# Norm and rotation of queries and keys made within the compression of cached keys, gates at the projection's head, shorter rings

## The reference

```python
def layer_forward(x, p_l, pos, z_prev0, wkv0, attend, lp):
    h = rmsnorm(x, lp['attn_norm'])
    z = h @ lp['w_in']
    o_r, wkv, shift = rwkv_mix(z[..., :RWKV_COLS], z_prev0, wkv0, lp)
    qn, qr, kvc, kvs, kvw, gates = nsa_project(z[..., RWKV_COLS:RWKV_COLS + NSA_COLS], pos, lp)
    o_n = attend(qn, qr, kvc, kvs, kvw, gates)
    ...
    x = x + peer_ffn(rmsnorm(x, lp['ffn_norm']), lp)

def nsa_project(zn, pos, lp):
    ...
    gates = jax.nn.sigmoid(zn[..., NSA_WIDTH + 6 * KV_WIDTH:].reshape(B, T, NSA_HEADS, N_NSA_BRANCH))
    qn = rmsnorm(q, lp['q_norm'])
    qr = rope(qn, pos)
    def prep(kvb, gk):
        return jnp.stack([rope(rmsnorm(kvb[:, :, 0], gk), pos), kvb[:, :, 1]], axis=2)
    return qn, qr, kv[:, :, 0], prep(kv[:, :, 1], lp['k_norm'][1]), prep(kv[:, :, 2], lp['k_norm'][2]), gates

def compress(kv_raw, lp):      # for the prompt's raw keys and values, and each sample's 1024 cached ones
    ...
    part = jnp.einsum('csekd,ersdf->crekf', chunks, w1)
    hid = part[0:nc, 0]
    for r in range(1, CMP_RATIO):
        hid = hid + part[r:r + nc, r]
    hid = jax.nn.gelu(hid + pe_bias[None, :, None, :])
    out = jnp.einsum('nekf,efd->nekd', hid, lp['cmp_w2'])
    kc = rmsnorm(out[:, 0], lp['k_norm'][0])
    return kc, out[:, 1], jnp.arange(nc) * CMP_STRIDE + CMP_BLOCK - 1
```

## Time and profile before

| | before |
|---|---|
| time, median of 3 runs | 3261.43 us (3260.53 to 3267.47) |
| the profiled execution | 3268.35 us |
| its span, first to last instruction | 3266.5 us |
| mean granted TensorE clock (share of full) | 0.894 |
| busy: PE, DVE, ACT, POOL | 84%, 45%, 31%, 27% |
| projection with gates | from 42 to 231 us |
| compression | 604 to 777 us |
| norm and rotation (`nsa_prepare_stage`) | 777 to 846 us |
| search | 1477 to 2067 us |
| experts | 2067 to 3137 us |
| collection | from 3137 us |

### The profile page before, as it was taken

How to read it: one execution, slowest core, us unless ns; L and a number is a source line. 1 busy time by engine, 2 the same in 40 slices (tenths; PEclk the granted TensorE clock), 3 DMA queues, 4 the chain that set the end, 5 groups by cost and what they waited for, 6 DMA issues and landing times. The chain is left out here.

```text
span 3266.5 us, 52655 instructions
## 1 busy us (share of the span) xinstructions
PE 2736.7 (84%) x20687; PEld 2293.1 (70%) x20687; DVE 1463.0 (45%) x3240; ACT 1012.3 (31%) x1840; POOL 878.2 (27%) x782
## 2 busy tenths in 40 slices
PE   5984877596796599869999978699989999999968
PEld 5983775585564498769999978466666667666647
DVE  3226442202563432347899955233433344344333
ACT  2102110111242202013443366344434444444431
POOL 0000000000000000000011175477656777767600
PEclk8976997698587699989999999799989999999979
DMA  3200000221310222016555535788978988989822
GB/s 104 83 18 6 4 4 34 99 59 59 104 36 5 65 77 77 26 52 208 186 186 185 187 137 197 270 303 313 316 277 286 324 318 320 328 290 325 300 86 69
DMA packets 204509, 516.23 MB, mean 158 GB/s; under 512 B 32002, under 2 KB 99074, under 8 KB 202306
## 3 DMA queue, kind: packets, MB, share of 16 engines
q1 hardware_dynamic: 147970, 345.18, 31.5%
q0 software_dynamic: 56320, 167.98, 14.7%
HBM read 466.27 MB, written 50.92 MB: 158 GB/s over the span
## 5 line engine op out<-in xcount | busy, mean ns | idle before, releaser
L2006 POOL TENSOR_TENSOR wide<-wide,sif 128x2048 f32<-128x2048 f32 (+1 forms) x10 | 52.8, 5279 | 1816.3 <-DVE wide L2122 1816.3
L2257 POOL DMA_INDIRECT dots<-dots,place x320 | 348.2, 1088 | 250.3 <-PE ps L2311 111.3
L1871 PE MATMUL ps<-h_hi,u_hi 128*128 128x320 f32 x1024 | 321.6, 314 | 8.4 <-DVE u_lo L2028 8.2
L2283 PE MATMUL ps<-h_hi,u_hi 128*128 128x256 f32 x1024 | 302.1, 295 | 23.5 <-issue 11.7
L1871 PE MATMUL ps<-h_lo,u_hi 128*128 128x320 f32 x1024 | 317.6, 310 | 0.0
L1871 PE MATMUL ps<-h_hi,u_lo 128*128 128x320 f32 x1024 | 317.4, 310 | 0.0
L2283 PE MATMUL ps<-h_lo,u_hi 128*128 128x256 f32 x1024 | 295.0, 288 | 20.9 <-issue 20.3
L2283 PE MATMUL ps<-h_hi,u_lo 128*128 128x256 f32 x1024 | 295.0, 288 | 16.3 <-issue 16.1
L2261 POOL DMA_INDIRECT v_row<-in_peer_v,expert x240 | 272.9, 1137 | 73.2 <-issue 73.2
L2283 PEld LDWEIGHTS ps<-h_hi,u_hi 128*128 128x128 f32 x1024 | 198.1, 193 | 105.3 <-issue 88.4
L2392 DVE TENSOR_TENSOR v_lo<-v_raw,v_hi 128x1024 fp32r<-128x1024 f32 x128 | 157.1, 1227 | 252.3 <-ACT v_hi L2341 137.6
(11 more groups left out here) (457 smaller groups left out, 5643.3 us busy)
## 6 DMA issues: line engine op xcount, KB each, us to landing
u_raw<-in_peer_u SPq DMA_DIRECT2D x256, 512.0 KB
v_raw<-in_peer_v SPq DMA_DIRECT2D x128, 512.0 KB
dots<-dots SPq DMA_DIRECT2D x128, 160.0 KB, 1.8
g<-gate_matrix SPq DMA_DIRECT2D x32, 512.0 KB
wt<-in_w_in SPq DMA_DIRECT2D x24, 512.0 KB, 3.6
pages<-in_cmp_pages SPq DMA_DIRECT2D x64, 128.0 KB, 2.1
kv_pages<-in_sel_pages SPq DMA_DIRECT2D x64, 128.0 KB, 2.1
wt<-in_w_zg SPq DMA_DIRECT2D x16, 512.0 KB, 3.7
```

The costliest lines, as they stand in the source:

```text
L1871: mm = nc.tensor.matmul(k.bank(j % 2, TX), lhs, r[:, c, TD:T], start=c == 0 and p == 0, stop=c == KD - 1 and p == 2)
L2006: nc.gpsimd.tensor_tensor(hot4, hot4, which, ALU.mult).then_inc(numbered, 1)
L2257: nc.gpsimd.indirect_dma_start(dots[:, s:s + 1], None, dots_flat, bass.IndirectOffsetOnAxis(f.place[:, s:s + 1], 0)).then_inc(d_got[s % SL ...
L2283: mm = nc.tensor.matmul(up_bank(j), lhs, r[:, c, 0:TD], start=c == 0 and n == 0, stop=c == KD - 1 and n == 2)
```

## The change

Three parts. (A) In `project_stage` the gates go to the head: VectorE rounds and splits their weights, TensorE makes 48 products of 288 columns with the gates' 24 columns as the stationary side into banks 6 and 7, ScalarE copies them to `g_rows`; behind the last tile five transposes bring them into place for the sigmoids. (B) `nsa_prepare_stage` is gone; its work is cut into pieces (a sum of a set; a spread, a turn, that is the rotation, of one tile; a value's transposes) that stand in the list `at_slot` of `compress_stage`: those of slot -1 ahead of the first slot, the others behind their slot. Pieces take the bank pairs 4-5 and 6-7 in turn; the compression's slots use two banks in place of four, its tail banks 2 and 3. Squares and scales lie in free tiles of z. The first-layer weights come in two halves, the copy of the window rows ahead of the third group of pages, the store of keys and values at the end. (C) Rings: `UTiles` holds three tiles in place of four, v two in place of four, the sparse tokens have 12 slots in place of 16, none of them in the place of x; so x stays where it is, and its store and load are gone.

```diff
-SLOTS = 16
-KEPT = 12
+SLOTS = 12
...
+            if gates is not None:
+                pe.wait_ge(gate_parted, 1)
+                for c in range(KD):
+                    for n, (lhs, r) in enumerate(three_passes(g_hi[:, c, :], g_lo[:, c, :], r_hi, r_lo)):
+                        for h in range(2):
+                            mm = nc.tensor.matmul(k.ps[0:NGATE, 6 + h, 0:TH], lhs, r[:, c, h * TH:(h + 1) * TH],
+                                                  start=c == 0 and n == 0, stop=c == KD - 1 and n == 2)
+                mm.then_inc(gate_mm, 1)
...
                 for tt in range(5):
                     n = min(P, T - tt * P)
-                    for c in range(KD):
-                        for r in (r_hi, r_lo):
-                            mm = nc.tensor.matmul(k.ps[0:n, 0, tt * NGATE:(tt + 1) * NGATE],
-                                                  r[:, c, tt * P:tt * P + n].bitcast(F32), gates[1][:, c, :],
-                                                  start=c == 0 and r is r_hi, stop=c == KD - 1 and r is r_lo)
-                mm.then_inc(gate_mm, 1)
+                    mm = nc.tensor.transpose(k.ps[0:n, 0, tt * NGATE:(tt + 1) * NGATE], g_rows[:, tt * P:tt * P + n],
+                                             k.ident[0:NGATE, 0:NGATE])
+                mm.then_inc(gate_turned, 1)
...
+    tiles = [ZQ, ZQ + 1, ZQ + 2, ZQ + 3, ZK + 2, ZK + 4]
+    sets = ((0, 4), (4, 2))
+    at_slot = {-1: [("sum", 0), ("value", 0), ("value", 1)] + [("spread", i) for i in range(4)],
+               4: [("sum", 1)], 6: [("spread", 4)], 7: [("spread", 5)], 9: [("turn", 4)], 10: [("turn", 5)]}
+    for i in range(4):
+        at_slot[i] = [("turn", i)]
...
+            for kind, i in at_slot[-1]:
+                piece(kind, i)
             for n in range(len(jobs) + 1):
                 for m in range(4):
                     if n < len(jobs):
                         first(n, m)
+                        for kind, i in at_slot.get(4 * n + m, ()):
+                            piece(kind, i)
...
-                    dst = k.ps[:, m, r * MAXW:r * MAXW + w]
+                    dst = k.ps[:, m % 2, r * MAXW:r * MAXW + w]
...
+            def invert(i):
+                dve.wait_ge(q_rooted, i + 1)
+                nc.vector.reciprocal(scale[i], scale[i]).then_inc(q_inverted, 1)
+            def piece_and_more(kind, i):
+                if kind == "spread" and i in (0, 4):
+                    invert(int(i == 4))
+                piece(kind, i)
...
-    SIZE = 4
+    SIZE = 3
...
-            sp.dma_start(k.x_dram, k.x.rearrange("p c t -> p (c t)")).then_inc(x_kept, 16)
...
-    RU, RV, RG, EG = us.SIZE, 4, 2, 4
+    RU, RV, RG, EG = us.SIZE, 2, 2, 4
...
-            sp.dma_start(k.x.rearrange("p c t -> p (c t)"), k.x_dram).then_inc(x_back, 16)
```

More of the change, by code:

```diff
@@ L1051, in compress_stage @@
     MAXW = SEQS * 2 * CH
+    tiles = [ZQ, ZQ + 1, ZQ + 2, ZQ + 3, ZK + 2, ZK + 4]
+    gains = [("q_norm", 0)] * 4 + [("k_norm", 1), ("k_norm", 2)]
+    sets = ((0, 4), (4, 2))
[3 more added lines that the diff above has]
+        at_slot[i] = [("turn", i)]
+    pieces = [(s, kind, i) for s in sorted(at_slot) for kind, i in at_slot[s]]
+    order = {(kind, i): n for n, (_, kind, i) in enumerate(pieces)}
     with ExitStack() as ctx:
@@ L1094, in _ @@
                                      landed[g % 2], 16)
+            sp.wait_ge(q_used, len(pieces))
+            sp.dma_start(k.d["out_kv"], Z[:, ZK:NZ, :].rearrange("p c t -> p (c t)")).then_inc(stored, 16)
+            sp.wait_ge(stored, 32)
         @block.tensor
         def _(pe):
-            pe.wait_ge(weights, 48)
+            pe.wait_ge(loaded, 32)
             def first(n, m):
@@ L1102, in first @@
                 e, f = m // 2, m % 2
+                if n == 0 and m == 0:
+                    pe.wait_ge(weights, 48)
+                if n == 0 and m == 2:
+                    pe.wait_ge(more, 16)
                 if m == 0:
@@ L1159, in _ @@
             last.then_inc(moved, 1)
+            for g, (at, m) in enumerate(sets):
+                for n in range(at, at + m):
+                    last = nc.scalar.activation(squares[n], Z[:, tiles[n], :], ACT.Square)
+                last.then_inc(q_squared, 1)
             def first(n, m):
@@ L1182, in tail_b, with piece @@
                 nc.scalar.activation(rs[:, 0:half], rs[:, 0:half], ACT.Sqrt).then_inc(rooted, 1)
-            steps(first, tail_a, tail_b)
+            def piece(kind, i):
+                if kind == "sum":
+                    act.wait_ge(q_mean, i + 1)
+                    nc.scalar.activation(scale[i], scale[i], ACT.Sqrt).then_inc(q_rooted, 1)
+            steps(first, tail_a, tail_b, piece)
         @block.vector
@@ L1225, in prompt_attention_stage @@
+            def invert(i):
[5 more added lines that the diff above has]
+                piece(kind, i)
+            dve.wait_ge(loaded, 32)
+            steps(first, tail_a, tail_b, piece_and_more)
 def prompt_attention_stage(k, cached):
```

235 lines of the change are left out of this document (117 added, 118 removed).

## The result

The changed kernel takes 3165.7 us (median of 5, 3149.8 to 3169.68) against 3260.53 of the kernel before beside it (3253.86 to 3267.47): a ratio of 0.970, 95% interval 0.967 to 0.973. It is 95 us faster. The forecast was 64 us faster, 3197.6, with a range down to 3170: the direction was right, the gain half as large again as forecast, and the time 4 us under the range.

What follows compares the result with a forecast made beforehand. TensorE, busy in 84% of the span, was taken as the bound, with time won where it waits or works slowly. Terms -21.6-36.6-6.6+1+0 = -63.8 took the median of 3261.43 to 3197.6 us; range 3170 to 3230.

Steps and rivals of the forecast that it cites:

- Gates: End of projection: ScalarE's 28.0 us idle goes, 48 matmuls ahead of the first tile cost 6.4; net -21.6 (-15 to -22).
- Compression: Compression and the stage behind it: 69.1 us come off, 32.5 are paid back; net -36.6 (-30 to -54).
- The first slot's place: Compression: copies, squares, sum, reciprocal and four spreads put the first slot at 631.8 in place of 619.03, +12.8 us.
- the hole at slot 6: Compression: TensorE waits 4.6 us ahead of spread 4 for VectorE's add and reciprocal and ScalarE's copy, with nothing covering it.
- rival (2): Compression: dense pieces ahead of the slots raise the clock, slots and turns run at 1.00, -17 us, about 3180; chance 0.16.
- The rule that was weighed there: Compression: continuous matmuls get TensorE past its slow clock, idle gaps bring it back; by it -54 in place of -36.6.
- Collection: Collection: without x asked for again, TensorE's wait for rows falls from 12.1 to 5.5 us; -6.6 (-5 to -8).
- Search: Search with three tiles of u: ScalarE starts 0.6 us late, covered by VectorE's split and TensorE's queue; +1 (0 to +5).
- Experts: Experts with twelve slots and two tiles of v: late gelu up to +35, smaller opening burst up to -10; 0 taken.
- the tight batches: Experts: one batch in five leaves 3.2 us for gathers to land before gelu; 35 us at most, 0 taken.
- the slots as a bound (4): Experts: every batch late because slots are retaken too slowly, 0.9 us a batch, about 3268 or more; chance 0.05.
- a chain that stays whole (5): Compression: pieces wait for one another on TensorE as before, rings take the rest; within 6.5 us of now; chance 0.02.

Runs made afterwards that it cites:

- The fourth experiment: The kernel before with 32 added unused products of 288 columns on TensorE ahead of the compression's first slot: first job's slots 14.40 us, compression with the stage behind it 227.98.
- the other trace of the unchanged stage: Trace of a kernel with other rings and an unchanged compression: compression with the stage behind it takes 239.23 us.
- the last experiment: Changed kernel with four tiles of u and reciprocals under slots, plus GpSimd's second and third opening batches waiting for TensorE's up products: ratio to before 0.963.

## Why the prediction was right and wrong

**Gates: right in the mechanism, a little past the end of the range.** -23.6 in the first trace, -27.1 and -23.2 in the changed kernel's other two, against -21.6 (-15 to -22). The gates took the slow part over, as forecast: 8.45 us for them, 2.7 less for the tiles, and 1.4 from the earlier start. In the trace with -27.1 every tile takes 6.24 us in place of 6.40; the second projection, which the change leaves alone, has a like step (105.0 for 107.4) in some traces of either program, so this is not the change's. The narrow stationary side raised the clock as the tiles had: it rose while the gates ran, in all traces of the changed kernel.

**Compression: the steps were right, the clock was not, and this made the prediction wrong.** The first slot's place (28.1 for 27.6) and the hole at slot 6 (4.68 for 4.6) came as worked out. Mis-sized were the slots, 27 us, and the turns, 7.06: together they were to take 34 and took 18.2 (a slot and its turn come every 4.54 us). The failed step is the sentence "I go by the row", by which the slots and turns were priced at the half clock. The row of 27 us at 0.50 was true of products that had found the clock at 0.50, behind a wait of 24 us; it said nothing of the same products behind dense work. The fourth experiment shows this with the kernel before alone, 14.40 us in place of 26.3. It was written down as rival (2), with its -54 for the stage, at a chance of 0.16; measured are -54.3 (-52 against the other trace of the unchanged stage). The 16 us of slots and turns are most of the difference to -36.6; the last 2 us lie within the 2.5 by which the unchanged stage differs between traces.

The rule that was weighed there (the Trainium skill, "TensorE: Matmul & The Clock Gate", section "Why this matters for your kernels") holds here in part. Its second half holds: a hole of 3.90 us ahead of the slots lost the clock. Its first half does not hold here as it stands: 26.3 us of narrow products without a hole did not raise the clock; they only kept it where dense work had raised it.

**Collection: right**, 5.96 us less of waiting, against 6.6.

**Search: mis-sized.** +1 (0 to +5) was forecast, +8.6 came, and with four tiles of u search is 6.4 to 9.6 us shorter in three traces. ScalarE's late rounding was covered for 104 steps, as worked out. The cover named, VectorE's split and TensorE's queue, is not there in the last 24 steps. There ScalarE also scales tiles for the experts' gates, and TensorE's wait for these grew by 7 of the 8.2 us that the 24 steps lost. That a rounding which starts late (1.74 us in the row above) pushes that scaling back is the likely link, argued from ScalarE's order and not shown by itself. I had read the cover from a mean over all steps.

**Experts: the middle of the range was wrong.** 0 (-10 to +35) was forecast. That the tight batches cost nothing was right: behind the first two batches, three gelus of 78 wait in this trace, 1.6 us in all. What was put at nothing wrongly is the opening, some 14 us shorter with 12 slots in the traces, where I allowed 10 and took none. What makes it shorter is not settled: the number of slots does it in both programs, the last experiment did not spread the burst, and the competition with the first loads is untried. That the later batches' order matters is unlikely, since the difference is there by step 3. The other part of this trace's -40.0, some 20 us in the rest of the stage, comes and goes between executions of the same kernel.

**Not forecast at all:** the recurrence (329 to 332 us in all traces with the change, 334 to 340 in those without) and prompt attention (mostly 6 us shorter), though no instruction of theirs changed. Why is open.

With these terms, each from traces (the opening's 14 a difference of means, not shown in the time), the sum is -23.6 - 54.3 - 6.0 + 8.6 - 14 - 6 - 3.5 = -99, against a measured -95 (by the interval of the ratio, -89 to -107). The rivals of the slots as a bound (4) and of a chain that stays whole (5) did not come.

## What to carry to other kernels

A row that says at which clock some products ran holds for what stood ahead of them: before costing products that a change moves behind other work, ask whether they are of the kind that raises the clock, or only keeps it. A cover is to be read in the stretch where it is used up last, not from a mean over the stage. And work that fills an engine's wait gains twice when it also closes the hole ahead of what follows; its own chains want a slot of other work between a slow step on one engine and its use on another.

## What the runs showed of the hardware

The same 64 products of 66 columns took 26.3 us at a granted 0.50 and 14.40 at 1.00, by what had stood ahead of them, and kept to either for nearly all their length; behind a hole of 3.90 us the clock was lost.

Prompt attention took 189.2 in all five traces of the kernel before and its variants, and 183.0 to 183.2 in seven of nine of the changed ones, with the same 768 matmuls; the windows of the two stretches:

```profile
845.87:1035.04 189.17, 163.69 (x768) 123.92 (x768) 104.59 (x453) 72.30 (x273) 0.00 (x0) 0.75 0.17 51
```

```profile
764.16:947.21 183.05, 156.96 (x768) 119.00 (x768) 104.36 (x452) 72.30 (x273) 0.00 (x0) 0.78 0.17 53
```

Its mean granted clock differs, 0.75 and 0.78, and in two changed traces, with 192.06 and 196.56, it was lower again (0.74 and 0.71). What differs is how long the clock stays at 0.50 from the stage's start: about 48 us in the trace of after, 54 in that of before, 55 and 60 in the two longest (196.56 and 192.06). A stage that wavers about the two levels gains or loses 3% by this; what decides when the clock rises is not shown.

One program's experts differ by 30 us from one execution to the next (1041 to 1072 in three traces of the changed kernel). In the openings TensorE has stretches of some 10 us in which it issues about a matmul a microsecond (7 in 10 us of the trace of after, 13 in 12 of that of before) and waits for nothing that the profile shows. Such idle time adds up to 20 to 23 us in the openings with 16 slots and 7 to 18 in those of the table with 12. What sets this idle time stays open.
